# A decoder layer with 64 routed experts: a shared product is split around the routing ranks, the first item's rows are turned one stage earlier, and the last items add their rows in another order

## The reference

```python
scores = sigmoid(xt @ w_router)
_, top_idx = top_k(scores + router_bias, 8)
gates = top_s / sum(top_s) * 2.5
# for every expert block of rows: gather its tokens, run the expert, scale by the gate
yb = swiglu(xt[tok_idx], w_gate_e[e], w_up_e[e], w_down_e[e]) * g[:, None]
routed = zeros_like(xt).at[src_tok].add(y_rows)
shared = swiglu(xt, w_gate_s, w_up_s, w_down_s)
return rmsnorm(h + routed + shared)[:, 16:]
```

## Time and profile before

| what | value |
|---|---|
| median of 3 runs | 1584.8 us (1584.04 to 1586.37) |
| the profiled execution, its own time | 1582.39 us |
| its span in the profile | 1580.5 us |
| PE busy | 1490.0 us (94%) |
| DVE busy | 922.1 us (58%) |
| POOL busy | 842.7 us (53%) |
| ACT busy | 584.0 us (37%) |
| mean granted TensorE clock | 0.98 of full speed |

### The profile page before, as it was taken

The page is one execution under the profiler, slowest core; times in us unless marked ns, Lnnn a source line. Parts: engine busy times, 40 slices in busy tenths (PEclk is TensorE's granted clock), DMA queues, the critical chain, the costliest instruction groups (busy, mean ns, idle before and its releaser), DMA issues.

```text
span 1580.5 us, 29151 instructions
## 1 busy us (share of the span) xinstructions
PE 1490.0 (94%) x9554; PEld 1273.0 (81%) x9554; DVE 922.1 (58%) x1595; ACT 584.0 (37%) x1052; POOL 842.7 (53%) x697
## 2 busy tenths in 40 slices
PE   6999999999979999979999999999999999999980
PEld 5799989899834675758999888999998889999970
DVE  3332788787867866444555555555556555555642
ACT  6433545444444231102333333333333333333333
POOL 0332153360601313345667777777777777778751
PEclk9999999999989999999999999999999999999995
DMA  5389521112070011436999999999999999999956
GB/s 188 95 264 303 185 80 43 63 60 73 28 294 31 17 54 54 161 118 226 334 330 337 325 329 330 328 336 341 340 328 329 329 330 340 329 334 331 329 153 229
DMA packets 104441, 356.77 MB, mean 226 GB/s; under 512 B 28191, under 2 KB 38404, under 8 KB 83406
## 3 DMA queue, kind: packets, MB, share of 16 engines
q1 hardware_dynamic: 60622, 246.60, 41.8%
q0 software_dynamic: 43776, 109.63, 26.0%
HBM read 300.68 MB, written 73.91 MB: 237 GB/s over the span
## 4 chain that ended last, share of the span: by engine, by line
POOL 20%; issue 17%; DMA 14%; PE 3%; POOLq 2%; DVE 0%; ACT 0%; SPq 0%; ACTq 0%; DVEq 0%
POOL wi L1636 17%; DMA acc_rows<-YE,sia 13%; POOL acc_rows L1649 2%; PE gu L1697 2%; POOL acc_rows L1654 1%; DMA A<-acc_rows 1%; POOLq L1636 0%; DVE XS L1833 0%; POOLq L1671 0%; POOLq L1652 0%; PE ype L1719 0%; PE yrest L1708 0%; ACT WH L1765 0%; PE ype L1721 0%; PE ype L1720 0%
## 5 line engine op out<-in xcount | busy, mean ns | idle before, releaser
L1697 PE MATMUL gu<-XS,place 128*128 128x160 f32 x4160 | 582.0, 301 | 8.7 <-DVE XS L1833 5.0
L1697 PEld LDWEIGHTS gu<-XS,place 128*128 128x128 f32 x4160 | 576.6, 191 | 16.1 <-DVE XS L1833 5.9
L1636 POOL DMA_INDIRECT wi<-xn_rows,gi x320 | 412.1, 1288 | 109.1 <-issue 97.3
L1838 DVE TENSOR_TENSOR WL<-place,WH 128x2048 fp32r<-128x2048 f32 x65 | 149.1, 2294 | 329.1 <-ACT WH L1765 189.1
L1833 DVE STREAM_TRANSPOSE XS<-wi 128x1280 f32<-128x1280 f32 x65 | 166.0, 2554 | 9.0 <-DMA wi<-xn_rows,tables 5.7
L1649 POOL DMA_INDIRECT acc_rows<-YF,sib x65 | 105.5, 1623 | 95.7 <-ACT YF L1774 73.4
L1123 POOL DMA_INDIRECT slot_table<-pay,si x64 | 62.4, 975 | 171.3 <-DVEq L1432 156.4
L1769 ACT ACTIVATE SS<-gu 128x160 f32<-128x160 f32 x130 | 39.5, 304 | 274.8 <-PE gu L1697 217.5
L1765 ACT ACTIVATE WH<-place 128x2048 fp32r<-128x2048 f32 x65 | 124.2, 1910 | 0.5 <-issue 0.5
L1654 POOL DMA_INDIRECT acc_rows<-YE,sia x65 | 102.7, 1580 | 20.4 <-issue 19.6
L1719 PE MATMUL ype<-WH,hidh 128*128 128x512 f32 x260 | 108.8, 419 | 0.0
(11 more groups left out here) (297 smaller groups left out, 2521.7 us busy)
## 6 DMA issues: line engine op xcount, KB each, us to landing
place<-in_w_gate_e SPq DMA_DIRECT2D x65, 1024.0 KB
place<-in_w_up_e SPq DMA_DIRECT2D x65, 1024.0 KB
place<-in_w_down_e SPq DMA_DIRECT2D x65, 1024.0 KB
place<-in_w_in POOLq DMA_DIRECT2D x16, 512.0 KB, 7.1
late_parts<-wq_parts POOLq DMA_DIRECT2D x8, 1024.0 KB, 6.1
late_parts<-xn_parts POOLq DMA_DIRECT2D x8, 1024.0 KB, 6.1
wf_parts<-late_parts POOLq DMA_DIRECT2D x8, 1024.0 KB, 5.1
w_low<-late_parts POOLq DMA_DIRECT2D x8, 1024.0 KB, 5.1
```

The costliest lines, as they stand in the source:

```text
L1636: pool.indirect_dma_start(XQ[q][:, s * DQ:(s + 1) * DQ], None, quarters_d, bass.IndirectOffsetOnAxis(ap=index[s], axis=0), bounds_check=QU ...
L1697: last = pe.matmul(gu[f][:, k, :], raw[:, t, f * P:f * P + P], XS[:, q, t, :], start=(t == 0), stop=(t == KT - 1))
L1838: tt(WL[q][:, :], WR[q][2][:, :], WH[q][:, :].bitcast(F32), ALU.subtract).then_inc(s_dlo, 1)
```

## The change

It has four parts.

1. **The output stage's order.** `ranks(7)` is issued after the first of the four parts of `hidden(5)`. The expert row product (L1267) goes ahead of `down(5)`, `hidden(7)` stands whole behind the table's transposes, and on DVE `accumulate(5)` stands behind the copies that repeat the table.
2. **Items 0 and 1 in the output stage.** POOL issues the gathers of both there. `XQ[1]` moves to the third stretch of the old slots, and the second stretch becomes `XS0`, the turned rows of item 0. So the writes of four tiles (2 to 5) must be done before the gathers. DVE turns item 0 between `accumulate(6)` and `accumulate(7)`. In the expert stage it turns only item 1 at the start.
3. **The expert stage's DVE and ACT.** `turned(n + 2)` goes ahead of `hidden(0, n + 1)`. ACT's `add_index(n)` waits on a new semaphore `s_free`, which POOL raises after its own wait on `s_ad`; it asks for the adds of items up to n - 2, in the last turns too.
4. **The last three items** (62 to 64) issue the transfer of `YE` first and that of `YF` behind it.

```diff
-    K.XQ = [slots[:, i * RUNS * DQ:(i + 1) * RUNS * DQ] for i in range(2)]
+    K.XQ = [slots[:, i * RUNS * DQ:(i + 1) * RUNS * DQ] for i in (0, 2)]
+    K.XS0 = slots[:, RUNS * DQ:2 * RUNS * DQ].rearrange("p (t c) -> p t c", t=KT)
+def turn_rows(nc, XS, XQ):
+    return nc.vector.transpose(XS.rearrange("p t (s j) -> p s t j", s=RUNS),
+                               XQ.rearrange("p (s i t) -> p s t i", s=RUNS, t=KT))
-        SLOT_TILES = (2, 3, 4)
+        SLOT_TILES = (2, 3, 4, 5)
 # POOL, output stage
-            for s in range(RUNS):
-                pool.indirect_dma_start(K.XQ[0]...).then_inc(K.s_g[0], 16)
+            for n in range(2):
+                for s in range(RUNS):
+                    pool.indirect_dma_start(K.XQ[n]...).then_inc(K.s_g[n], 16)
 # PE, output stage
             logits(TT - 1)
-            hidden(TT - 3)
+            hidden_free(TT - 3)
+            hidden_part(TT - 3, 0)
             ranks(TT - 1)
+            for part in range(1, 4):
+                hidden_part(TT - 3, part)
             down(TT - 4)
...
             hidden(TT - 2)
-            down(TT - 3)
             pe.wait_ge(s_row, 1)
             pe.matmul(op[0][0:1, 0:ITEMS], exf[0:ITEMS, :], ...).then_inc(s_er, 1)
-            hidden_free(TT - 1)
-            hidden_part(TT - 1, 0)
-            hidden_part(TT - 1, 1)
+            down(TT - 3)
...
-            hidden_part(TT - 1, 2)
-            hidden_part(TT - 1, 3)
+            hidden(TT - 1)
             down(TT - 2)
             down(TT - 1)
 # DVE, output stage
             shared_hidden(TT - 2)
-            accumulate(TT - 3)
             dve.wait_ge(s_er, 1)
...
+            accumulate(TT - 3)
             dve.wait_ge(s_tp, 1)
...
             accumulate(TT - 2)
+            dve.wait_ge(K.s_g[0], 16 * RUNS)
+            turn_rows(nc, K.XS0, K.XQ[0]).then_inc(K.s_xk, 1)
             accumulate(TT - 1)
 # POOL, expert stage
+            def rest_rows(n, q):
+                pool.wait_ge(s_yk, n + 2)
+                pool.sem_inc(turn["pool"], 1)
+                pool.indirect_dma_start(acc_q, ..., YF[q][:, :], None, compute_op=ALU.add, ...).then_inc(s_ad, 16)
+            def add_rows(n, q, ending):
+                if not isinstance(n, int) or n > 0:
+                    pool.wait_ge(s_ad, n * 32)
+                    pool.sem_inc(s_free, 1)
+                pool.wait_ge(s_si, n + 1)
+                pool.sem_inc(turn["pool"], 1)
+                if not ending:
+                    rest_rows(n, q)
+                pool.wait_ge(s_ya, n * 2 + 4)
+                pool.sem_inc(turn["pool"], 1)
+                pool.indirect_dma_start(acc_d, ..., YE[q][:, :], None, compute_op=ALU.add, ...).then_inc(s_ad, 16)
+                if ending:
+                    rest_rows(n, q)
-            gather_runs(1, [K.quart[:, RUNS + s:RUNS + s + 1] for s in range(RUNS)])
+            pool.sem_inc(s_free, 2)
 # ACT, expert stage
-            def add_index(q, n, added):
-                if added is not None:
-                    act.wait_ge(s_ad, added)
-                    act.sem_inc(turn["act"], 1)
+            def add_index(q, n):
+                act.wait_ge(s_free, n + 1)
+                act.sem_inc(turn["act"], 1)
 # DVE, expert stage
                 low_down(q, n)
-                if ahead >= 1:
-                    hidden(0, o, n + 1)
                 if ahead >= 2:
                     turned(q, n + 2, i * LANDED + 2 * LANDED)
                 if ahead >= 1:
+                    hidden(0, o, n + 1)
                     hidden(1, o, n + 1)
-            for q in two:
-                turned(q, None, LANDED)
+            turned(1, None, LANDED)
```

More of the change, by code:

```diff
@@ L95, in setup @@
     K.s_ao = ctx.enter_context(nc.semaphore("acc_written"))
+    K.s_xk = ctx.enter_context(nc.semaphore("x_turned"))
     K.WR = [[K.place[:, (3 * i + k) * KT * FF:(3 * i + k + 1) * KT * FF] for k in range(3)] for i in range(2)]
@@ L1131, in _ @@
             quarters_d = xn2_d.rearrange("r (b n) -> (r b) n", b=QUARTERS)
-            for s in range(RUNS):
-                pool.indirect_dma_start(K.XQ[0][:, s * DQ:(s + 1) * DQ], None, quarters_d,
-                                        bass.IndirectOffsetOnAxis(ap=K.quart[:, s:s + 1], axis=0)).then_inc(K.s_g[0], 16)
+            for n in range(2):
+                for s in range(RUNS):
+                    pool.indirect_dma_start(K.XQ[n][:, s * DQ:(s + 1) * DQ], None, quarters_d,
+                                            bass.IndirectOffsetOnAxis(ap=K.quart[:, n * RUNS + s:n * RUNS + s + 1], axis=0)).then_inc(K.s_g[n], 16)
             pool.wait_ge(s_ti, 16)
@@ L1537, in phase_experts @@
         XQ = K.XQ
-        XS = sb("XS", [P, 2, KT, CAP])
+        XS = [K.XS0, sb("XS1", [P, KT, CAP])[:, :, :]]
         SS = sb("SS", [P, 2, CAP])
@@ L1556, in phase_experts @@
         s_g = K.s_g
-        s_ad = sem("rows_added")
-        s_xk = sem("x_turned")
+        s_ad, s_free = sem("rows_added"), sem("rows_free")
+        s_xk = K.s_xk
         s_gu, s_gk = sem("gate_up_done"), sem("gate_up_used")
@@ L1661, in turn_ @@
                     gather(q, n + 4)
-                add_rows(n, q)
-            gather_runs(1, [K.quart[:, RUNS + s:RUNS + s + 1] for s in range(RUNS)])
+                add_rows(n, q, ahead < 2)
+            pool.sem_inc(s_free, 2)
             for q in two:
@@ L1696, in gate_up @@
                     for t in range(KT):
-                        last = pe.matmul(gu[f][:, k, :], raw[:, t, f * P:f * P + P], XS[:, q, t, :], start=(t == 0), stop=(t == KT - 1))
+                        last = pe.matmul(gu[f][:, k, :], raw[:, t, f * P:f * P + P], XS[q][:, t, :], start=(t == 0), stop=(t == KT - 1))
                 last.then_inc(s_gu, 1)
@@ L1779, in evict, with turn_ @@
                 act.activation(YE[q][:, 512 * g:512 * g + 512], yp[g][:, :], ACT.Copy, scale=K.gate[0][:, bass.ds(n, 1)]).then_inc(s_ya, 1)
-            def turn_(i, q, ahead, added):
+            def turn_(i, q, ahead):
                 n = i * 2 + q
@@ L1789, in turn_ @@
                 if ahead == 1:
-                    high_down(1 - q, n + 1, i + 2)
+                    high_down(1 - q, n + 1, i + (q + 1))
                 if ahead >= 1:
                     sigmoid(1, n + 1)
-                add_index(q, n, added)
+                add_index(q, n)
                 evict_rest(q, n)
@@ L1803, in _ @@
             for q in two:
-                turn_(0, q, 3, None)
-            with act.Fori(0, last - 1) as i:
+                turn_(0, q, 3)
+            with act.Fori(1, last) as i:
                 for q in two:
[L1807 to L1810, removed]
+                    turn_(i, q, 3)
+            turn_(last, 0, 2)
+            turn_(last, 1, 1)
+            turn_(last + 1, 0, 0)
             act.activation(rt[:, 0:1], K.eps[:, 0:1], ACT.Sqrt).then_inc(s_r, 1)
@@ L1832, in turned @@
                 dve.sem_inc(turn["dve"], 1)
-                nc.vector.transpose(XS[:, q, :, :].rearrange("p t (s j) -> p s t j", s=RUNS),
-                                    XQ[q].rearrange("p (s i t) -> p s t i", s=RUNS, t=KT)).then_inc(s_xk, 1)
+                turn_rows(nc, XS[q], XQ[q]).then_inc(s_xk, 1)
             def low_down(q, n):
```

## The result

The changed kernel takes 1576.8 us (median of 8 runs, 1572.24 to 1580.53) beside 1584.5 us for the kernel before on the same chip: ratio 0.995, 95% interval 0.9938 to 0.9963, so 7.7 us faster. Its runs spread over 8.3 us, those of the kernel before over 2.6. The profiled execution took 1578.9 us, 2.1 above the median.

What follows compares the result with a forecast made beforehand. The prediction took the loop to be bound by PE. Its terms, -1.6 - 1.3 + 1.0 - 5.9 = -7.8, took the profiled 1582.39 to 1574.6, plus 2.4 for the median: 1577.0 us, range 1571.5 to 1582.5.

Steps and rivals of the forecast that it cites:

- Term 1: Output stage's end: gate_up of item 0 starts at 701.6 instead of 703.19, -1.6 us.
- Term 2: Item 0's gate_up: less PE idling ahead of it, so a higher granted clock; half of 2.7 taken, -1.3 us.
- term 3: Loop: ACT waits on POOL's count instead of the adds themselves, a hop costing +1.0 us (0 to +3.7).
- term 4: The end: ACT leaves the chain of waits, three rounds take 22.6 us instead of 28.6, -5.9 us.
- the rule weighed against it: At the end: a transfer's semaphore lands only behind the same DMA engine's earlier writes, so YE first buys nothing by itself.
- The ranks step: Output stage: last ranks start after one 1.85 us part of hidden(5), so place(7) comes at about 656.5, 6.2 earlier.
- ten gathers end near 699.7, POOL and DVE tie: Output stage's end: ten gathers end at 699.7 and DVE's last half at about 699.8.
- The stall of 7.24: Behind item 0's gate_up: a 7.24 us stall without a cause found in the trace, carried over unchanged.
- The rival that it shrinks: Stall behind item 0's gate_up loses some 4 of 7 us and the clock holds: 1571, chance 12%.
- hidden(6) ends at 676.6: Output stage: PE's end of hidden(6), from which the expert product and down(5) were counted to 680.9 to 681.3.
- The slower rival, ACT behind POOL: Loop: the hop delays high_down and stalls PE, from 0.20 us a turn; +3.2 us, 1588, chance 8%.
- It does nothing measurable: Whole kernel: output stage gains nothing, loop costs 3.7, end gives -4.4; about -1 us, 1584, chance 8%.

Runs made afterwards that it cites:

- front_only: Kernel before with only the output stage's new order, both items' gathers and item 0's turning moved there; loop and end unchanged: 1588.4 us, ratio 0.9995.
- tail_only: Kernel before with only ACT's wait on s_free and the new transfer order of the last three items: 1581.6 us, ratio 0.9958.
- tail_rest_first: Kernel before with only ACT's wait on s_free; YF's transfer stays ahead of YE's in the last items: 1585.3 us, ratio 0.998.
- after: The changed kernel itself, all four parts, against the kernel before: 1576.8 us, ratio 0.995; its profiled execution took 1578.9 us.
- order_only: Kernel before with only the new order of PE and DVE in the output stage: 1588.4 us, ratio 0.9996.
- gathers_apart: Changed kernel with item 1's gathers back at the expert stage's start and those of items 2 and 3 held until item 0's gate_up is done: 1580.2 us, 0.9962.
- late_gathers: Changed kernel with the gathers of items 2 and 3 held until item 0's gate_up is done: 1586.7 us, ratio 0.9995 against the kernel before.
- spaced: item1_back with waits on PE's progress ahead of the gathers of items 2, 3 and 4: 1571.7 us, ratio 0.9931 against the kernel before.
- spaced_direct: spaced, with ACT in the loop waiting on the landed adds themselves instead of POOL's count: 1572.2 us, ratio 0.9931 against the kernel before.
- item1_back: Changed kernel with item 1's gathers back at the expert stage's start, fifteen in a row, no new wait: 1577.1 us, ratio 0.9956 against the kernel before.

## Why the prediction was right or wrong

The forecast was 1577.0 and the median is 1576.8; on another chip the gain was 4.4, which would be 1580. The sum is right, but not for all of its reasons, and that it is right to 0.2 us is luck: the -2.9 of terms 1 and 2 didn't come (front_only: 0.9995), nor is the +1.0 of term 3 shown. What carries the result is term 4, by itself 6.6 us in tail_only.

**Term 4 (the end, -5.9): right.** The table has -6.03. The rounds were forecast at 22.6 and are 22.8: 8.66, 8.02 and 6.08. The first two are longer than 7.5, since YF takes 5.64 and 5.06 from issue to landing, not 4.64; the last is shorter, as YF of the nearly empty item takes 2.73. So the mechanism is right, and that the three add up to the forecast is two errors that cancel. In tail_rest_first a round is 1.15 + 1.87 + 6.2 = 9.2, as the rows show it (1532.10 to 1541.32). What YF's new place saves is its issue, 1.87, ahead of the longest transfer. As to the rule weighed against it (the Trainium skill, DMA: Bandwidth & Descriptors, Queues, rings and completion order): the trace doesn't contradict it. YF lands 7.5, 6.9, 6.3 and 6.7 behind YE's issue (after, then tail_only, the first two rounds of each), never ahead of the 6.2 at which YE would land. But "the new order buys nothing by itself" doesn't follow from it: the order is worth 3.5 us (tail_only beside tail_rest_first), because the shorter transfer's issue no longer stands ahead of the longer one.

**Term 1 (earlier gate_up of item 0, -1.6): wrong.** The ranks step was too optimistic: part 0 of hidden(5) took 3.07 at a granted clock of 0.64, not 1.85, and DVE began place(7) only 2.1 us behind the ranks' end, so it moved by 2.8 against logits(7), not by 6. The table read moved by 2.6. The next step hid this: the first gather waits for tile 5's write and came 1.25 earlier, for which I had 1.1. What failed is "ten gathers end near 699.7, POOL and DVE tie". The ten gathers end at 702.2 (48.6 behind logits(7), for which I had 48.8), but DVE's last half ends 57.9 behind logits(7), for which I had 48.9. Three things make up most of that: hidden(7) takes 9.32 and not "7.5 us", its signal is 4.5 late, and down(7), after 5.32 of idle PE, takes 5.25 on a lowered clock instead of 3.60. The first of them comes with the new order, as order_only has it too (9.27), though not in every trace: gathers_apart has 7.32 at the full clock. gate_up of item 0 starts 6.75 later against logits(7), not 1.6 earlier.

**Term 2 (clock, -1.3): not shown as a gain.** gate_up of item 0 does run at the full clock now, 8.93 at a granted 1.00, as against 0.66 in the earlier trace rows. But the low clock only moved ahead, to hidden(7) (a mean of 0.77) and down(7) (0.83 over 702 to 712), and in front_only and late_gathers, with the same front, item 0's gate_up takes 10.61 at 0.84.

**The stall of 7.24, "I find no cause for it in the trace and carry it over unchanged": the step of the front that failed.** It goes with POOL's row of issues, not with PE's place in the code: late_gathers moved it to item 2, and spaced took it out. The rival that it shrinks was half right. Held are 4.5 us at hidden(7) and 2.3 in item 1's gate_up (721.36 to 732.53, where it has 8.85 without a stall), in place of the 7.24. A form of it stood in the earlier trace rows already: "hidden(6) ends at 676.6" has 2.7 us of it inside. What the shorter stall gives back, the stage's end costs: front_only is at 0.9995.

**Term 3 (+1.0): the size fits (+1.35), the cause isn't shown; luck.** front_only, in which ACT waits on the adds directly, has 786.97 from down_rest(0) to down_rest(62), more than the 785.55 of the changed kernel; spaced and spaced_direct have 785.42 and 785.54. The turn stays at 12.64. PE's idle time between 740 and 1500 grew from 0.04 to 0.59, and where it lies differs from run to run. The slower rival, ACT behind POOL, is out: it needed 0.20 us a turn.

**"It does nothing measurable"** was right for the front, of which only the order and the whole were run by themselves.

**What stays open.** How POOL holds PE. Whether the pause, the number of issues or something of PE's own decides wasn't separated; the scatters, if theirs is the same stall, show that neither ten issues nor much data is needed. Code loading, the other candidate, fits badly: in the kernel before an instruction transfer does start between 715 and 717, where the stall begins, but gathers_apart has none between 721 and 737, though its item 2 breaks up from 728.6 to 733.5, spaced has three between 719 and 725 while its rows stay whole, and in the kernel before none starts between 664 and 686, though hidden(6) breaks up from 673 to 676. What sets an execution's drift before the edits isn't known, nor why the changed kernel's runs spread so widely (8.3 us, while spaced spreads over 1.7).

## What to carry to other kernels

When the trace shows a stall in which an engine stops for "issue" or "remote" and another one goes on issuing, look for the stall wherever that other engine does the same, and suspect its work before moving more of it to a place where others wait. Work moved earlier is only earlier if its signal is. In a chain of dependent transfers, take every engine out of the round that needn't be there, and issue the longest transfer first: two small edits gave the 6.6 us (tail_only) that a rebuilt stage didn't. And one trace of each kernel isn't enough for a stretch whose length differs by 3 us between traces of the same code.

## What the runs showed of the hardware

While POOL issues indirect transfers one after another (one per 1.26 to 1.31 us), and most of all late in a row of ten or more gathers, PE's finished work is reported late, and PE takes up new work in small pieces that start 0.7, 1.4 or 2.1 us apart. The last piece starts 1.5 to 2.5 us behind the end of the last scatter or gather, with eight scatters as with ten or fifteen gathers. A late report came from 3.6 us before to 2.3 us behind the last gather's end, and in spaced once while the row went on. In rows of five with none close ahead it was 0 to 1.4 us late:

| kernel | gathers in a row | last ends | PE's work ended | seen by ACT |
|---|---|---|---|---|
| order_only, output stage | 5 | 694.1 | 695.58 | 695.62 |
| spaced, item 0 | 5 | 711.1 | 713.33 | 713.37 |
| tail_only, hidden(7) | 5 | 698.8 | 694.50 | 694.53 |
| spaced_direct, hidden(7) | 5 | 694.3 | 694.00 | 695.40 |
| after, hidden(7) | 10 | 702.2 | 696.70 | 701.19 |
| after, item 0 | 10 | 726.4 | 721.52 | 726.54 |
| late_gathers, hidden(7) | 10 | 702.2 | 695.66 | 698.64 |
| item1_back, item 0 | 15 | 725.3 | 714.56 | 726.62 |
| gathers_apart, down_rest(0) | 15 | 732.0 | 724.31 | 733.60 |
| spaced, down_rest(0) | 5 and 5, 1.4 apart | 729.4 | 727.19 | 730.45 |
| spaced, down_rest(1) | 5, then adds and gathers | goes on | 739.83 | 745.01 |

In the first two lines the work ended behind the row, so they show only that the delay doesn't outlast it. In the loop POOL issues five gathers and two adds to a turn and the turn stays at 12.64. At the end, behind the last gathers, an accumulating transfer of 512 KB (YE) lands 6.0 to 6.5 us after its issue, and in the loop, where the DMA share is 1.00, it took 9.6 (after) and 10.5 (before) in the chains of waits; one for a nearly empty item takes 4.3 to 4.6 as YE and 2.7 to 2.8 as YF.
